# A two-layer hybrid decoder on one core: the first MLP's up half as seven block products, and its modulation vectors summed beside the first stages

## The chip, the cores and the metric

The kernel runs on one core of one Trainium2 chip. The metric is the device time of one execution in microseconds (us), the median of several. TensorE (PE in the profile) does the matrix products; VectorE (DVE), ScalarE (ACT) and GpSimd (POOL) work on its results; SyncE (SP) issues most of the DMAs. Each engine works through its own list of instructions in order and waits on semaphores for the others.

## The reference

One sequence of 1024 tokens of width 1024 goes through two layers. Cut to what matters here (`modulate` is x * (1 + scale) + shift):

```python
cs = silu(c)
sh_m, sc_m, g_m, sh_f, sc_f, g_f = split(cs @ ada_w[layer] + ada_b[layer], 6)
kv_shift, kv_scale = split(cs @ kv_ada_w + kv_ada_b, 2)          # once, for the shared K and V
# layer 0: y = mlstm_mixer(modulate(h, sh_m, sc_m)); layer 1: y = sliding-window attention over shared K and V
h = layer_norm(ALPHA * h + (1 + g_m) * y, ln_g[2 * layer], ln_b[2 * layer])
u = modulate(h, sh_f, sc_f)
y = square(relu(u @ mlp_w_up[layer])) @ mlp_w_down[layer]        # 1024 -> 4096 -> 1024
h = layer_norm(ALPHA * h + (1 + g_f) * y, ln_g[2 * layer + 1], ln_b[2 * layer + 1])
```

Fourteen vectors of 1024 entries come out of the `cs @ ada_w` products: six for each layer (named SH_M0 ... G_F0 and SH_M1 ... G_F1) and SH_KV and SC_KV for the shared K and V.

## The kernel before

**Products.** Every fp32 product is done as three products of rounded parts: high by high, high by low, low by high (`product`, L2670 to L2672). So each operand is split into a high part (ACT, L964 for weights) and a low part (DVE, L1609 for weights: the whole less the high part).

**Stages, in order.** A start; the q and k projection; the projection to v (16 tiles of 24 products, "V tiles", evacuated by DVE in `evac_v`, L1761, from a ring of three PSUM banks); the o projection with the mLSTM chunks between, whose first state product is L2914; the mixer's output (out0, out1); the first MLP (MLP0); K and V (KV); q and attention; the attention's output (op0, op1); the second MLP (MLP1).

**The two MLPs.** Each goes through the 4096 inner columns in 8 chunks of 512. Chunk 0 is done plainly: 8 up groups of 24 products and 16 down groups of 12. For the other chunks the matrices are cut into 2 by 2 blocks and multiplied with seven block products in place of eight (P1 to P7; their operands are sums and differences of blocks). MLP1 does so in the up half and in the down half (`both_chunk`, 168 + 168 products; its last chunk has plain downs), with the low parts of the summed u operands stored in DRAM and fetched back through a ring (`ulo_dram`). MLP0 does so in the down half alone (`seven_chunk`, 192 + 168 products in chunks 1 to 6), and its chunk 7 is plain.

**Vectors.** A vector needs eight row blocks of `ada_w` (512 KB each), which SP fetches into one of two slots of `stage`; DVE adds each, times its entry of cs, to `acc` (`ada`, L1567 and L1571: one of them is called an ada here), and PE then sums over the partitions (`sum_vector`, or `sum_quarters`, L2695, and `turn_quarters` in MLP0); `take_mod` (L1591) reads the sum. Weights pass through the same two slots of `stage`, in one order (`load_order`). Three vectors are summed beside the q, k and v projections (SH_F0, SC_F0, SH_KV), two in the mixer's later stages (G_M0, G_F0), and the seven others beside MLP0's chunks 0 to 6. A slot comes free when the piece in it has been used on DVE, and only then does SP issue its next load.

**Attention.** It goes through 16 pairs p. For each, DVE reads the sums of the exponentials (`totals`, L2308 and L2309, twice for each pair), POOL scales the probabilities (L890), and PE transposes them (L3149). For p of 8 and more DVE also does `affine_kv` (L2323, L2324: the norm's row times and plus a tile of the residual).

**Last chunk of MLP1.** The row `ln_b` is added to the tiles of the residual: to four by POOL (L923) during the ups, to four by DVE (L2650) during the downs. In MLP0 the row is added in chunk 0 by DVE (`affine`, L1981 and L1982).

## Time and profile before

| | before |
|---|---|
| median of 3 runs | 2147.69 us (2147.02 to 2148.5) |
| the profiled execution | 2148.5 us, its span 2146.8 us |
| PE busy | 2100.7 us, 98% of the span |
| DVE busy | 1502.8 us, 70% |
| ACT busy | 882.8 us, 41% |
| POOL busy | 270.6 us, 13% |
| mean granted clock of TensorE | 0.997 |

The span is the profiled stretch from the first to the last instruction; every start time below is counted from its beginning. A row of the timeline gives the start, the duration, engine, line, operation, result and operands, the number of instructions, and in brackets the idle time of the engine before it with what ended it. A result in PSUM is written by PE, and the engine that reads it frees the bank.

### The profile page before, as it was taken

What the parts mean: (1) busy time and instruction counts of PE and PEld (TensorE: products, weight loads), DVE (VectorE), ACT (ScalarE), POOL (GpSimd) and SP (SyncE); (2) the same over time, 40 slices, a digit from 0 to 9 for tenths busy, and PEclk for the clock granted to TensorE, in tenths of its full rate; (3) what the DMA queues carried; (4) which work ended last, traced back from release to release, by engine and by line L of the source; (5) the groups of instructions that cost most, each with busy time, mean ns of one, the idle gap of its engine ahead of it and who ended that gap; (6) DMA issues with size and microseconds to landing.
All of it is one profiled execution on the core that took longest, in us unless ns stands there. A gap on an engine that the chain in (4) does not pass through costs nothing.

```text
span 2146.8 us, 28666 instructions
## 1 busy us (share of the span) xinstructions
PE 2100.7 (98%) x9816; PEld 1702.2 (79%) x9816; DVE 1502.8 (70%) x2343; ACT 882.8 (41%) x1529; POOL 270.6 (13%) x248
## 2 busy tenths in 40 slices
PE   6999999999999999999999999999999999999998
PEld 5888888878888888888888777678787888888886
DVE  7423666678676676776768665767788788778878
ACT  4201454162234233342337455655434434534552
POOL 0000220010010110110100023232000011011034
PEclk9999999999999999999999999999999999999999
DMA  7434643303424224224121210211345433533531
GB/s 298 137 102 126 124 94 139 126 20 120 126 69 137 97 79 137 78 83 147 34 98 72 79 30 11 79 58 42 124 182 185 162 131 137 205 114 121 195 137 79
DMA packets 77315, 242.16 MB, mean 113 GB/s; under 512 B 8417, under 2 KB 8593, under 8 KB 73649
## 3 DMA queue, kind: packets, MB, share of 16 engines
q1 hardware_dynamic: 69376, 219.18, 30.1%
q0 software_dynamic: 5088, 17.48, 3.7%
q10 hardware_dynamic: 2768, 4.41, 0.5%
q8 instruction: 50, 0.82, 0.2%
q14 instruction: 33, 0.26, 0.0%
HBM read 225.29 MB, written 15.76 MB: 112 GB/s over the span
## 4 chain that ended last, share of the span: by engine, by line
PE 84%; DVE 7%; DMA 4%; ACT 3%; issue 2%; POOL 1%; SPq 0%; DVEq 0%; ACTq 0%; POOLq 0%
PE ps L2670 25%; PE ps L2672 25%; PE ps L2671 25%; DMA stage<-in_stream 3%; PE ps L3135 1%; PE ps L3165 1%; PE ps L3149 1%; DVE wlo L1609 1%; ACT whi L964 1%; PE ps L2914 1%; PE ps L2773 1%; PE ps L2899 1%; DMA early_place<-in_early 1%; PE ps L2903 1%; DVE stats L1918 1%
## 5 line engine op out<-in xcount | busy, mean ns | idle before, releaser
L2672 PE MATMUL ps<-uhi,wlo 128*128 128x512 f32 x760 | 296.4, 390 | 0.0
L2670 PE MATMUL ps<-whi,uhi 128*128 128x512 f32 x704 | 287.6, 408 | 0.2 <-ACT resid L1309 0.2
L2670 PE MATMUL ps<-uhi,whi 128*128 128x512 f32 x704 | 276.3, 392 | 5.9 <-DVE wlo L1609 3.2
L2672 PE MATMUL ps<-whi,ulo 128*128 128x512 f32 x704 | 275.4, 391 | 0.0
L2671 PE MATMUL ps<-wlo,uhi 128*128 128x512 f32 x704 | 274.8, 390 | 0.0
L2671 PE MATMUL ps<-ulo,whi 128*128 128x512 f32 x704 | 274.8, 390 | 0.0
L2672 PEld LDWEIGHTS ps<-uhi,wlo 128*128 128x128 f32 x760 | 143.1, 188 | 29.8
L2670 PEld LDWEIGHTS ps<-uhi,whi 128*128 128x128 f32 x704 | 132.6, 188 | 37.0 <-DVE wlo L1609 4.6
L2670 PEld LDWEIGHTS ps<-whi,uhi 128*128 128x128 f32 x704 | 132.5, 188 | 36.6 <-issue 10.0
L2672 PEld LDWEIGHTS ps<-whi,ulo 128*128 128x128 f32 x704 | 132.2, 188 | 28.9
L2671 PEld LDWEIGHTS ps<-ulo,whi 128*128 128x128 f32 x704 | 132.5, 188 | 27.2
L2671 PEld LDWEIGHTS ps<-wlo,uhi 128*128 128x128 f32 x704 | 132.6, 188 | 24.9
L2107 DVE TENSOR_TENSOR resid<-ps,resid 128x512 f32<-128x512 f32 x168 | 112.4, 687 | 50.9 <-PE ps L2672 50.9
L964 ACT ACTIVATE whi<-stage 128x1024 fp32r<-128x1024 f32 x76 | 79.3, 1053 | 148.5 <-DMA stage<-in_stream 54.2
L1609 DVE TENSOR_TENSOR wlo<-stage,whi 128x1024 fp32r<-128x1024 f32 x76 | 92.8, 1230 | 65.7 <-ACT whi L964 65.3
L1571 DVE SCALAR_TENSOR_TENSOR acc<-stage,cs,acc 128x1024 f32<-128x1024 f32 x84 | 107.6, 1281 | 43.5 <-DMA stage<-in_stream 42.3
L2471 DVE TENSOR_TENSOR resid<-ps,resid 128x512 f32<-128x512 f32 x168 | 109.2, 681 | 11.3 <-PE ps L2672 10.7
L1219 ACT ACTIVATE h_blocks<-ps 128x512 f32<-128x512 f32 x48 | 28.6, 595 | 211.6 <-PE ps L2672 211.6
L2670 PE MATMUL ps<-whi,hhi 128*128 128x512 f32 x288 | 113.1, 393 | 0.2
L2671 PE MATMUL ps<-wlo,hhi 128*128 128x512 f32 x288 | 112.1, 389 | 0.0
L2672 PE MATMUL ps<-whi,hlo 128*128 128x512 f32 x240 | 93.5, 389 | 0.0
L866 POOL TENSOR_TENSOR whi<-w_whole,wlo 128x1024 fp32r<-128x1024 f32 x12 | 28.9, 2407 | 496.2 <-DVE hhi L2071 486.1
(437 smaller groups left out, 4614.6 us busy)
## 6 DMA issues: line engine op xcount, KB each, us to landing
stage<-in_stream SPq DMA_DIRECT2D x248, 512.0 KB, 3.6
hlo<-ulo_dram SPq DMA_DIRECT2D x28, 1024.0 KB, 4.8
ulo<-ulo_dram SPq DMA_DIRECT2D x20, 1024.0 KB, 5.3
w_whole<-in_stream SPq DMA_DIRECT2D x14, 512.0 KB, 5.2
aux<-in_early SPq DMA_DIRECT2D x8, 512.0 KB, 7.5
...
```

The costliest lines, as they stand in the source:

```text
L866: pool.tensor_tensor(w_part(lo), w_block(lo), fr(w_part(hi)), ALU.subtract).then_inc(w_low_by_pool, 1)
L964: act.activation(whi[:, slot_of(w), :], stage[:, n % 2, :], ACT.Copy).then_inc(hi_ready, 1)
L1219: act.activation(block, ps[:, g % RING, :], ACT.Relu).then_inc(act_evac, 1)
L1571: ins = v.scalar_tensor_tensor(acc[:], stage[:, n % 2, :], cs[:, 0, k:k + 1], acc[:], ALU.mult, ALU.add)
L1609: v.tensor_tensor(wlo[:, slot_of(w), :], stage[:, n % 2, :], fr(whi[:, slot_of(w), :]), ALU.subtract).then_inc(loads_used, 1)
L1918: return v.bn_stats(stats[:, t % 2, 6 * half:6 * half + 6], resid[:, t, half * HALF:(half + 1) * HALF])
L2107: v.tensor_tensor(dst, ps[:, bank, :], dst, ALU.add).then_inc(dve_evac, 1)
L2471: v.tensor_tensor(dst, ps[:, down_bank(first, product, t), :], dst, ALU.add).then_inc(dve_evac, 1)
L2670: pe.matmul(dst, left_hi, right_hi, start=start, stop=False, skip_group_check=more)
L2671: pe.matmul(dst, left_hi, right_lo, start=False, stop=False, skip_group_check=more)
L2672: return pe.matmul(dst, left_lo, right_hi, start=False, stop=stop, skip_group_check=more)
L2773: last = pe.transpose(ps[:, X + n % 4, k * P:(k + 1) * P], src[:, at:at + P], ident[:])
```

## The change

1. **MLP0 by seven products in both halves.** MLP0's chunks 1 to 6 are done by the code of MLP1 (`both_chunk`, now with the MLP's number m as an argument), and chunk 7 has seven-product ups and plain downs as in MLP1. The stores and ring loads of `ulo_dram` and the four-part loads of blocks are issued by SP in MLP0 too. `seven_chunk`, `sum_quarters` and `turn_quarters` are gone.
2. **Vectors.** SH_F0, SC_F0 and SH_KV are summed beside the blocks 7 to 13 of the weights (during the q and k projection); SC_KV, SH_M1, SC_M1 and G_M1 beside the V tiles 1 to 15, two adas in a tile (three, three and two in the last tiles); SH_F1 and SC_F1 one ada in every V tile, whose pieces are fetched to a buffer of their own (`scratch`, one slot, with its own semaphores `side_in` and `side_used`), called side loads here; G_F1 beside the second half of the o projection. Every vector is summed with `sum_vector`.
3. **First chunks of the MLPs.** The weights come in the order 2, 3, 4, 5, 6, 7 (before: 4, 5, 2, 3, 6, 7), the first of them right behind the square of the third up group.
4. **Modulations.** `angles` and the modulations 2 to 4 move from MLP0's end to the first tiles of out1.
5. **Attention.** The first `totals` of each pair stands ahead of `affine_kv`.
6. **P2's weight.** In every `both_chunk` the low part of P2's weight (`both_up_low`) stands ahead of the gates 0 and 1 (a gate multiplies a block of the down weight by the gate row).
7. **The row ln_b.** POOL adds it to all eight tiles in the last chunk of both MLPs.

The core of the diff:

```diff
+SIDE = (SH_F1, SC_F1)
+BESIDE_QK = {7: [(SH_F0, 0, 3)], 8: [(SH_F0, 3, 6)], 9: [(SH_F0, 6, 8)], 10: [(SC_F0, 0, 4)], 11: [(SC_F0, 4, 8)],
+             12: [(SH_KV, 0, 4)], 13: [(SH_KV, 4, 8)]}
+BESIDE_V = {t: (v, 2 * n, 2 * n + 2) for first, v in ((1, SC_KV), (5, SH_M1), (9, SC_M1)) for n, t in
+            enumerate(range(first, first + 4))}
+BESIDE_V.update({13: (G_M1, 0, 3), 14: (G_M1, 3, 6), 15: (G_M1, 6, 8)})
-CHUNK_LOADS = [4, 5, 2, 3, 6, 7, 8, 9]
+CHUNK_LOADS = [2, 3, 4, 5, 6, 7]
+LOADS_AT = {2: (2,), 3: (3, 4), 4: (5,), 5: (6,), 6: (7,)}
...
+            def load_one(n):
+
+                sp.wait_ge(loads_used, n - 1)
+                sp.dma_start(stage[:, n % 2, :], stream[n]).then_inc(stage_loaded[n % 2], 16)
+
+            def load_side(n):
+
+                if n:
+                    sp.wait_ge(side_used, n)
+                else:
+                    sp.wait_ge(gate_m, 6)
+                sp.dma_start(scratch[:].rearrange("p a n -> p (a n)"), stream[SIDE_BASE + n]).then_inc(side_in, 16)
+
+            load_pairs(2, IN_V, 0)
+            load_side(0)
+            tile = 1
+            for n in range(IN_V, AFTER_V):
+                load_one(n)
+                while tile < 2 * T and n + 1 >= LOADED_THROUGH[tile - 1]:
+                    load_side(tile)
+                    tile += 1
+            load_pairs(AFTER_V, N_EARLY, 0)
...
-            for t in range(T):
-                adas(SC_F0, range(t, t + 1))
-                if t == T - 1:
+            for tile in range(2 * T):
+                nh, t = divmod(tile, T)
+                if tile == T - 1:
                     preps(14, 15)
-                evac_v(0, t)
-            for t in range(T):
-                evac_v(1, t)
-                adas(SH_KV, range(t, t + 1))
...
+                evac_v(nh, t)
...
+                ada(SIDE[nh], t)
+                if tile in BESIDE_V:
+                    adas(*BESIDE_V[tile])
...
-                if p >= T:
-                    affine_kv(p - T)
                 if more:
                     totals(2 * p + 2)
+                if p >= T:
+                    affine_kv(p - T)
+                if more:
                     totals(2 * p + 3)
...
-            mlp_chunk(FIRST["mlp0"], W_MLP0, 0, with_ada=True, head=lambda t: normed(TR_LN0, 0, t))
-            with pe.Fori(0, len(SEVEN)) as i:
-                seven_chunk(chunk_start(FIRST["mlp0"], 1), W_MLP0 + 8, 0, i, 16, True)
+            def mlp_through(m, tail=None):
+
+                mlp_chunk(m)
+                with pe.Fori(0, len(SEVEN)) as i:
+                    both_chunk(m, both_start(FIRST[MLP[m]], 1), 0, i)
+                first = both_start(FIRST[MLP[m]], CHUNKS - 1)
+                both_chunk(m, first, len(SEVEN), 0, last=True)
```

How the instructions stand now. The first place is DVE in the V tiles of before: between two evacuations (L1761) stands one ada (L1571), which reads a slot of `stage`.

```order
L1761 COPY resid<-ps 128x2x256
L1571 SCALAR_TENSOR_TENSOR acc<-stage,cs,acc 128x1024
L1761 COPY resid<-ps 128x2x256
L1571 SCALAR_TENSOR_TENSOR acc<-stage,cs,acc 128x1024
L1761 COPY resid<-ps 128x2x256
```

The same place of the changed kernel, where the evacuation is L1743, an ada L1556 or L1560, and the second vector's total lies in `gate_row`:

```order
L1743 COPY resid<-ps 128x2x256
L1570 TENSOR_TENSOR mods<-ps,mods 128x8
L1560 SCALAR_TENSOR_TENSOR acc<-scratch,cs,acc 128x1024
L1560 SCALAR_TENSOR_TENSOR gate_row<-stage,cs,gate_row 128x1024 x2
L1743 COPY resid<-ps 128x2x256
L1560 SCALAR_TENSOR_TENSOR acc<-scratch,cs,acc 128x1024
L1560 SCALAR_TENSOR_TENSOR gate_row<-stage,cs,gate_row 128x1024 x2
```

Between two evacuations there now stand three adas: one that reads the side load (`scratch`) and two that read the slots of `stage`.

On SP the loads of this stretch were one loop over pairs of `stage` loads. In the changed kernel they are written out behind that loop, from V tile 1 on:

```order
L708 DMA scratch<-in_stream 128x1024
L700 DMA stage<-in_stream 128x1024 x2
L708 DMA scratch<-in_stream 128x1024
L700 DMA stage<-in_stream 128x1024 x2
L708 DMA scratch<-in_stream 128x1024
```

So one side load follows each two `stage` loads, in one queue; a side load waits until the side piece before it is used, and a `stage` load until its slot is free.

The second place is DVE in the pair p = 8 of attention, before: the low parts of two weights, `affine_kv` (L2323, L2324), then `totals` twice (L2308, L2309) and the low part of the output (L2316).

```order
L1609 TENSOR_TENSOR wlo<-stage,whi 128x1024 x2
L2323 TENSOR_TENSOR resid<-resid,lnrows 128x1024
L2324 TENSOR_TENSOR resid<-resid,acc 128x1024
L2308 TENSOR_TENSOR att<-att 128x4
L2309 RECIPROCAL att<-att 128x4
L2308 TENSOR_TENSOR att<-att 128x4
L2309 RECIPROCAL att<-att 128x4
L2316 TENSOR_TENSOR ulo<-ps,uhi 128x4x128
```

The same pair of the changed kernel:

```order
L1588 TENSOR_TENSOR wlo<-stage,whi 128x1024 x2
L2399 TENSOR_TENSOR att<-att 128x4
L2400 RECIPROCAL att<-att 128x4
L2414 TENSOR_TENSOR resid<-resid,lnrows 128x1024
L2415 TENSOR_TENSOR resid<-resid,acc 128x1024
L2399 TENSOR_TENSOR att<-att 128x4
L2400 RECIPROCAL att<-att 128x4
L2407 TENSOR_TENSOR ulo<-ps,uhi 128x4x128
```

The first of the two `totals` has moved ahead of `affine_kv`, the second has stayed behind it.

The third place is DVE in MLP1's chunk 0, before: behind each square (L1997) the weight's scaling (L1604), the low part of the up group (L2001), the low part of a weight (L1609) and a row of the residual (L2611). The weights are 4 and 5; weight 2, which the fifth up group needs, comes right behind these rows.

```order
L1997 TENSOR_TENSOR h_whole<-h_whole 128x512
L1604 TENSOR_TENSOR stage<-stage,gate_row 128x1024
L2001 TENSOR_TENSOR hlo<-h_whole,hhi 128x512
L1609 TENSOR_TENSOR wlo<-stage,whi 128x1024
L2611 TENSOR_TENSOR resid<-resid,lnrows 128x1024
L1997 TENSOR_TENSOR h_whole<-h_whole 128x512
L1604 TENSOR_TENSOR stage<-stage,gate_row 128x1024
L2001 TENSOR_TENSOR hlo<-h_whole,hhi 128x512
L1609 TENSOR_TENSOR wlo<-stage,whi 128x1024
L2611 TENSOR_TENSOR resid<-resid,lnrows 128x1024
L1997 TENSOR_TENSOR h_whole<-h_whole 128x512
L2001 TENSOR_TENSOR hlo<-h_whole,hhi 128x512
```

The same place of the changed kernel, where the square is L1985 and the low part of a weight L1588:

```order
L1985 TENSOR_TENSOR h_whole<-h_whole 128x512
L1992 TENSOR_TENSOR hlo<-h_whole,hhi 128x512
L2235 TENSOR_TENSOR resid<-resid,lnrows 128x1024
L1985 TENSOR_TENSOR h_whole<-h_whole 128x512
L1992 TENSOR_TENSOR hlo<-h_whole,hhi 128x512
L2235 TENSOR_TENSOR resid<-resid,lnrows 128x1024
L1985 TENSOR_TENSOR h_whole<-h_whole 128x512
L1588 TENSOR_TENSOR wlo<-stage,whi 128x1024
L1992 TENSOR_TENSOR hlo<-h_whole,hhi 128x512
```

Weight 2 is now the first of the chunk, behind the third square, and the two scaled weights have moved behind it.

## Rows read from the trace of the kernel before

**Rows 1.** The page, busy time of the engines, share of the span
```profile
PE 2100.7 (98%) x9816; PEld 1702.2 (79%) x9816; DVE 1502.8 (70%) x2343; ACT 882.8 (41%) x1529; POOL 270.6 (13%) x248
```

**Rows 2.** Windows: PE, PEld, DVE, ACT, POOL busy (instructions), granted clock, DMA share, GB/s
```profile
129.88:221.24 91.36, 90.58 (x415) 75.10 (x414) 35.32 (x41) 8.39 (x18) 2.80 (x4) 1.00 0.41 121
466.00:1117.91 651.91, 649.56 (x2909) 531.94 (x2909) 461.49 (x559) 220.62 (x296) 62.09 (x33) 1.00 0.31 98
1498.51:2110.22 611.71, 604.86 (x2656) 497.34 (x2657) 492.28 (x541) 277.61 (x358) 64.90 (x35) 1.00 0.42 149
```

**Rows 3.** Timeline of PE: chunk starts in MLP1 and MLP0
```profile
1749.88 0.39 PE L2670 MATMUL ps<-uhi,ninth 128*128 128x512 f32 x1
1826.14 0.39 PE L2670 MATMUL ps<-uhi,ninth 128*128 128x512 f32 x1
...
714.11 0.64 PE L2695 MATMUL ps<-acc,ones 128*32 128x256 f32 x8
797.01 0.64 PE L2695 MATMUL ps<-acc,ones 128*32 128x256 f32 x8
```

**Rows 4.** Timeline and window of MLP1's chunk 0
```profile
1525.88 1.23 DVE L1609 TENSOR_TENSOR wlo<-stage,whi 128x1024 fp32r<-128x1024 f32 x1 [0.25 <-ACT whi L964]
...
1527.16 0.50 PE L2670 MATMUL ps<-uhi,whi 128*128 128x512 f32 x1 [2.75 <-DVE wlo L1609]
...
1527.16:1531.60 4.44, 4.44 (x12) 3.53 (x13) 3.49 (x4) 1.58 (x2) 0.00 (x0) 0.62 0.40 122
```

**Rows 5.** Timeline and window of attention's pair 8
```profile
1358.43 1.22 DVE L2323 TENSOR_TENSOR resid<-resid,lnrows 128x1024 f32<-128x1024 f32 x1
1359.68 1.23 DVE L2324 TENSOR_TENSOR resid<-resid,acc 128x1024 f32<-128x1024 f32 x1
...
1363.22 1.09 PE L3149 MATMUL ps<-ident,probs 128*128 128x128 f32 x8 [3.13 <-POOL probs L890]
...
1363.22:1368.60 5.38, 5.38 (x24) 3.67 (x26) 2.58 (x15) 1.17 (x3) 2.40 (x2) 0.68 0.13 25
```

**Rows 6.** Timeline of DVE: four adas in a row, then a V tile
```profile
97.43 1.28 DVE L1571 SCALAR_TENSOR_TENSOR acc<-stage,cs,acc 128x1024 f32<-128x1024 f32 x1
100.99 1.28 DVE L1571 SCALAR_TENSOR_TENSOR acc<-stage,cs,acc 128x1024 f32<-128x1024 f32 x1 [2.28 <-DMA stage<-in_stream]
103.19 1.28 DVE L1571 SCALAR_TENSOR_TENSOR acc<-stage,cs,acc 128x1024 f32<-128x1024 f32 x1 [0.91 <-DMA stage<-in_stream]
105.83 1.28 DVE L1571 SCALAR_TENSOR_TENSOR acc<-stage,cs,acc 128x1024 f32<-128x1024 f32 x1 [1.36 <-DMA stage<-in_stream]
...
141.11 0.70 DVE L1761 COPY resid<-ps 128x512 f32<-128x512 f32 x1 [3.56 <-PE ps L2672]
```

**Rows 7.** The tile stage, 90 to 130 us: its loads, issue to landing
```profile
DMA to landing us min/median/max: 3.4/3.5/4.3
```

**Rows 8.** Timeline of PE: a vector's sum, and the first state product
```profile
128.18 1.84 PE L2687 MATMUL ps<-ones,acc 128*128 128x1 f32 x16
129.88 0.49 PE L2670 MATMUL ps<-whi,uhi 128*128 128x512 f32 x1
...
228.41 0.70 PE L2914 MATMUL ps<-resid,ktok 128*128 128x257 f32 x2 [0.26 <-DVE mods L1591]
```

**Rows 9.** Waits of PE: result, line, what ended them, total, times, longest
```profile
PE ps L2670 <- DVE h_blocks L2441: 1.3, 2, 0.8
...
PE ps L2670 <- DVE spare_r L2411: 0.7, 1, 0.7
...
PE ps L2670 <- DMA ulo<-ulo_dram: 0.5, 1, 0.5
```

**Rows 10.** Timeline of POOL and DVE in MLP1's last chunk
```profile
2068.52 12.55 POOL L923 TENSOR_TENSOR resid<-resid,lnrows 128x1024 f32<-128x1024 f32 x4 [7.11 <-ACT lnrows L1453]
...
2079.33 2.83 DVE L2411 TENSOR_TENSOR whi<-w_whole,hhi 128x1024 fp32r<-128x1024 f32 x1
...
2090.08 1.22 DVE L2452 TENSOR_TENSOR hhi<-h_blocks,wlo 128x1024 fp32r<-128x1024 f32 x1
```

1642 lines of the change are left out of this document (707 added, 935 removed).

## The prediction

> **What bounds the kernel now.** The first view was the page: PE is busy for 98% of the span, no other engine for more than 70% [rows 1]. So the time is PE's instructions plus its few waits, and a change pays by products removed or waits removed. Next came the windows of the stages: in MLP0, in MLP1 and in the V tiles PE is busy all the time but for a few us [rows 2]. Then the waits of PE one by one: most are under 1 us [rows 9], two are near 3 us [rows 4, 5]. Last I read DVE and the loads where the change adds work [rows 6, 7], since there PE's cover decides.
>
> **MLP0.** A product starts each 76.26 / 336 = 0.227 us: in MLP1 a chunk of 336 products lasts from 1749.88 to 1826.14. In MLP0 a chunk of 360 lasts 82.90 us (714.11 to 797.01) [rows 3]; 24 products are 5.45 us of the 6.64 between, the vector's quarter sums the rest, 1.2 us. Chunks 1 to 7 lose 24 products each: 168 × 0.227 = 38.1 us, and chunks 0 to 6 their sums, 7 × 1.2 = 8.4 us: 46.5. A direct comparison says the same with MLP1's stalls in it: from the first product to the end of the third tile of the last downs MLP0 takes 651.91 us, MLP1, which is what MLP0 becomes, 611.71 [rows 2]. MLP1's number holds 4.6 us that the change removes (next part): 607.1. Term: **−44.8 us**. The change to P2's order concerns the entry from chunk 0 to chunk 1: there PE waits 0.7 us for a weight's low part, then 0.5 for a ring load, then up to 0.8 for an addition of DVE [rows 9]. The first goes away; but the ring load is issued by PE's progress and lands no earlier, so the next wait takes it over. I count 0 in either MLP, bounds −1.5 and +1.5.
>
> **MLP1's chunk 0.** PE waits 2.75 us for weight 2's low part, and its next 12 products take 4.44 us at a granted clock of 0.62 where 12 × 0.227 = 2.7 would do [rows 4]. In the new order DVE has four instructions of 1.22 us less ahead of that low part, and needs only about 3.4 us to be in time. Term: −2.9 − 1.7 = **−4.6 us**; the bound above is 0.
>
> **Attention, pair 8.** DVE does `affine_kv` (1.22 + 1.23 us) ahead of `totals`; PE waits 3.13 us for the probabilities, and the next 5.38 us run at 0.68, which costs 5.38 × 0.32 = 1.7 us [rows 5]. With `totals` ahead, 2.4 us of the wait go and, the wait being short then, I take it that the clock stays up. Term: **−4.1 us**; bounds −4.8 and −2.4.
>
> **The vectors beside q, k and V.** This is where time is given back. *PE's part:* a vector's sum takes 129.88 − 128.18 = 1.70 us [rows 8]; eleven are made where there were four, six of the seven new ones ahead of the first state product (L2914 at 228.41 [rows 8]), which gives +10.2, and one in out0, +1.7. *The loads' part:* before, each V tile has one ada, and DVE waits 3.56 us for PE in a tile [rows 6]. After, a tile has two adas from `stage`, one from the side buffer. Where before four adas follow each other, DVE waits for the loads: two adas start each 105.83 − 100.99 = 4.84 us [rows 6], because a slot must be used, then filled (3.5 us from issue to landing [rows 7]). So two loads need 4.84 us of the 5.45 of a tile, and everything else that passes through `stage` comes on top. I count the chain from 97.43, behind the low part of weight 10: 19 `stage` loads up to weight 13 and the last of SH_KV, 37 from there to weight 18, 56 × 2.42 = 135.5 us; eight of them are weights, whose slot is held until ACT's high part (1.05 us) and DVE's low part are made, about +1.16 each, 9.3; and about 4.6 us from the last weight's landing to the state product, for DVE's and ACT's other work. That gives 97.4 + 149.4 = 246.8. The side load stands in the same queue and shares the DMA engines; where loads follow each other closely their landing rises from 3.5 to 4.3 us [rows 7], so each of 15 side loads may delay the others by 0 to 0.8 us: 246.8 to 258.8. I take the middle, 252.5: **+24 us** against 228.41. The bounds: +10.2 (PE alone binds), and +36 (landing at 4.3 for each pair, and a little of DVE's order lost). The Trainium skill ("DMA: Bandwidth & Descriptors", Anatomy of one DMA — SWDGE (gpsimd) path) has 2.0 us + bytes / 436e3 for one DMA, an estimate of 3.2 us for 512 KB. By that rule only 1.2 us of a load is transfer and a third load in flight costs next to nothing, so the stretch would end at 246.8, 6 us sooner. The trace's 3.5 us is near the rule, its 4.3 speaks against the second half of it.
>
> **The clock in that stretch.** A PE that waits for loads may wait 3 us or more at a time; after the two waits of that size the clock fell for 4.4 and 5.4 us at a cost of 1.7 each [rows 4, 5]. I count two such: **+3.5 us**, bounds 0 and +10.
>
> **The adds on POOL.** While POOL does its four adds (12.55 us), DVE's additions of two SBUF operands take 2.83 us where they take 1.22 soon after [rows 10]. Now eight adds stand in the last ups of both MLPs. Each further add costs DVE about 1.6 us, 4 × 1.6 = 6.4 us in MLP1, and in MLP0 as much beyond what the 611.71 holds, and DVE's idle time beside the ups and the four adds that it loses hide most. I take 1.5 us for each: **+3 us**, bounds 0 and +10. The Trainium skill ("SBUF — State Buffer", Terms) calls the port pair of DVE and GpSimd exclusive, held for the full instruction; the trace agrees, 2.83 against 1.22 us. By it all of the 6.4 us is lost where DVE has no idle time, +12.8 for both, which would make the sum 10 us longer.
>
> **At no cost:** the modulations in out1 and the first chunk's other moves, behind which DVE waits for PE in each tile; if that cover were gone, a modulation would be worth 1 to 2 us once. The copy in place of a zeroed state is as long.
>
> **Sum,** against the profiled execution's own 2148.5 us: −44.8 −4.6 −4.1 +24 +1.7 +3.5 +3 = −21.3, so 2127.2. The median of the runs shown is 0.8 lower than that execution: **2126.4 us**, 1.0% faster.
>
> **The rivals.** *(a) The loads fit under PE.* If a side load hides wholly and the weights' stage time overlaps, the stretch costs PE's sums alone, +10.2 and no clock loss: 2126.4 − 13.8 − 3.5 = 2109. For it: 4.84 us for two loads is under 5.45. Against it: the weights and the long runs of four adas in the q and k projection, where before already DVE waits for loads. Chance 0.13. *(b) The stretch is much slower.* Landing at 4.3 or more with three loads in flight, DVE's order holding up PE, more clock loss: +36 and +7, 2142. Chance 0.12. *(c) POOL's lock.* By the rule above all of DVE's lost time shows: 2136. Chance 0.08. *(d) The other side: the side loads run in series with the stage loads.* SP issues in order; a side load waits until DVE has used the one before, and DVE uses it only behind an evacuation that waits for PE. If so each stage load behind it starts only then, and a tile needs three loads in turn, 3 × 2.42 = 7.3 us or more: 71 loads × 2.42 = 172 + 13.9, the state product at 283, +55, 2157. Against it: when a side load is issued, its slot was freed a tile before, at the head of DVE's adas. It decides from about 6.7 us per V tile (16 tiles × 1.3 = 21 us, which eats the gain). Chance 0.04. *(e) The change of P2's order and POOL's eight adds do nothing at all:* 2123, inside my own range. Chance of my case (2119 to 2134): 0.63.
>
> **How the numbers follow.** The forecast is the likeliest, 2126. Leaving out the ends of (a) and (b), the range 2110 to 2140 holds 8 in 10: its low end is (a), its high end takes in (c) and most of (b); my own case has 2119 to 2134. A measurement of this kernel can tell about 0.2%, 4.3 us. Faster (under 2143.4): cases (a), (c), mine and most of (b), 0.93; within 0.2%: 0.03, from the end of (b); slower: 0.04, case (d).
>
> **What would show each step.** MLP0 from first product to the third tile's end near 607 us, chunks at 76.3; no wait for weight 2 in MLP1's chunk 0; at pair 8 a wait under 1 us and a clock of 1.0; the first state product between 245 and 259, with PE waits in the V tiles that end in DVE's copy or adas, and DVE waits that end in `stage` or `scratch` DMA; V tiles of 6 us rather than 5.45; DVE's additions at 2.8 us for some 25 us in both last ups. The prediction is wrong above all if the V tiles take 5.5 us or over 6.7.

## The result and the profile after

The changed kernel takes 2197.18 us (median of 4 runs, 2193.72 to 2201.87), the kernel before 2148.1 us beside it (4 runs): a ratio of 1.0229, interval 1.0209 to 1.0249. It is 2.3% slower; forecast was 2126, 1.0% faster. Two executions with a lower granted clock and a much longer time, one of e2's (3923.67 us) and one of the kernel before (3542.37 us), are left out of every number.

The page of the changed kernel, its first part, to be set beside [rows 1]:

```profile
span 2195.5 us, 28565 instructions
PE 2092.7 (95%) x9676; PEld 1691.5 (77%) x9676; DVE 1617.8 (74%) x2406; ACT 942.2 (43%) x1594; POOL 302.1 (14%) x255
```

PE is busy for 8 us less in a span 48.7 us longer: PE stands idle longer, and behind its waits products run at a lower granted clock. The waits of PE (total us, how often, the longest one) name where; [rows 9] has those of before:

```profile
PE ps L2509 <- DVE h_blocks L2065: 18.7, 24, 1.7
PE ps L2529 <- DVE gate_row L1560: 15.9, 3, 10.8
PE ps L2697 <- DVE resid L1743: 5.9, 1, 5.9
PE ps L2966 <- DVE att L2383: 5.3, 6, 2.6
PE ps L2509 <- DVE wlo L1588: 5.0, 3, 2.1
PE ps L2599 <- DVE qk L1783: 3.1, 2, 2.4
PE ps L2529 <- DVE acc L1560: 2.9, 1, 2.9
```

`L2509` with `h_blocks` is mostly the group of products P6 (one of the seven of an up half), `L2529` a vector's sum, `L2697` a group of transposes whose bank a V tile's evacuation has yet to free. All the releasers are DVE instructions, none is a load; what DVE itself waited for has to be read from its own timeline.

To divide the 48.7 us, I took the start of one instruction at the edge of each stage in both traces (us from the start of the span):

| stage, up to | before | after | the stage is longer by | forecast |
|---|---|---|---|---|
| q/k projection: first product of V tile 0 | 129.88 | 132.91 | +3.0 | 0 |
| V tiles: first state product | 228.41 | 277.74 | +46.3 | +24 with the clock's +3.5 apart |
| mLSTM chunks: first transpose for the o projection | 330.09 | 380.03 | +0.6 | 0 |
| o projection: MLP0's first product | 466.00 | 531.52 | +15.6 | +1.7 |
| MLP0: first transpose of the KV stage | 1168.88 | 1203.83 | −30.6 | −44.8, adds +1.5 |
| KV stage: first score | 1230.43 | 1265.40 | 0.0 | 0 |
| attention: MLP1's first product | 1498.51 | 1537.63 | +4.2 | −4.1 |
| MLP1: last matmul | 2137.20 | 2185.93 | +9.6 | −4.6, adds +1.5 |

Every stage that holds a part of the change comes out worse than its term.

**The V tiles.** PE's timeline: the first product of V tile 0, the three longest waits (in brackets), and the first state product:

```profile
132.91 0.49 PE L2509 MATMUL ps<-whi,uhi 128*128 128x512 f32 x1
154.93 3.57 PE L2529 MATMUL ps<-ones,gate_row 128*128 128x1 f32 x16 [10.84 <-DVE gate_row L1560]
241.94 3.57 PE L2529 MATMUL ps<-ones,gate_row 128*128 128x1 f32 x16 [4.44 <-DVE gate_row L1560]
265.04 2.07 PE L2697 MATMUL ps<-qk 128*128 128x128 f32 x8 [5.85 <-DVE resid L1743]
277.74 0.70 PE L2742 MATMUL ps<-resid,ktok 128*128 128x257 f32 x2 [0.26 <-DVE mods L1570]
```

DVE's timeline in and around it (the number before `DMA` is DVE's idle time):

```profile
126.11 1.28 DVE L1560 SCALAR_TENSOR_TENSOR acc<-stage,cs,acc 128x1024 f32<-128x1024 f32 x1 [6.66 <-DMA stage<-in_stream]
153.59 1.28 DVE L1560 SCALAR_TENSOR_TENSOR gate_row<-stage,cs,gate_row 128x1024 f32<-128x1024 f32 x1 [1.48 <-DMA stage<-in_stream]
154.79 0.68 DVE L1743 COPY resid<-ps 128x512 f32<-128x512 f32 x1
198.49 1.23 DVE L1588 TENSOR_TENSOR wlo<-stage,whi 128x1024 fp32r<-128x1024 f32 x1 [3.98 <-ACT whi L1000]
254.98 1.28 DVE L1560 SCALAR_TENSOR_TENSOR gate_row<-stage,cs,gate_row 128x1024 f32<-128x1024 f32 x1 [6.86 <-DMA stage<-in_stream]
```

The ada of 153.59 is the last piece of SH_KV, and V tile 0's evacuation (`L1743`) stands directly behind it. PE stood for 10.84 us ahead of SH_KV's sum; that the sum itself then lasts 3.57 us where it takes 1.70 [rows 8] is the clock's price. The waits of 6.66 and 6.86 us have a neighbour: POOL fetches `decay_rows` and `dmat` just ahead of both (the first pair, POOL's timeline) in pieces of 512 bytes. The 6.86 us lie ahead of PE's wait of 5.85.

```profile
114.06 0.80 POOL L847 DMA_DIRECT2D decay_rows<-rows_dram  x1 [2.48 <-DMA rows_dram<-winter]
114.85 0.76 POOL L847 DMA_DIRECT2D dmat<-rows_dram  x1
```

The windows of the V stretch and of the o projection (length, busy time of PE, PEld, DVE, ACT, POOL, granted clock, DMA share, GB/s):

```profile
132.91:277.74 144.83, 118.57 (x539) 98.98 (x538) 86.74 (x91) 12.93 (x27) 5.34 (x6) 0.88 0.73 230
380.03:531.52 151.49, 142.09 (x661) 116.88 (x660) 100.73 (x190) 53.83 (x100) 10.28 (x23) 0.97 0.34 107
```

PE is idle for 26.3 us in the first, where the 98.53 us of before held 1.1 us of waits in all. Its mean clock is 0.88, and a part of the waits is paid again in slower products: PE's busy time grew by 21.1 us (97.49 before), five more sums at 1.70 us [rows 8] are 8.5 of it, and the other 12.6 us are an estimate of what the lower clock cost. In the second stretch PE is idle for 9.4 us; the longest waits are these (and two for `wlo`, 1.02 us at 480.61 and 1.83 us at 484.10):

```profile
421.50 1.85 PE L2599 MATMUL ps<-ident,qk 128*128 128x128 f32 x8 [2.40 <-DVE qk L1783]
444.40 2.54 PE L2529 MATMUL ps<-ones,acc 128*128 128x1 f32 x16 [2.93 <-DVE acc L1560]
```

**Attention, pair 8.** The wait of [rows 5], 3.13 us, is down to 1.66, and others stand beside it. POOL, DVE and PE:

```profile
1393.85 2.79 POOL L938 TENSOR_TENSOR probs<-probs,att 128x1024 f32<-128x1024 f32 x1 [5.54 <-DVE att L2400]
1393.67 1.21 DVE L2414 TENSOR_TENSOR resid<-resid,lnrows 128x1024 f32<-128x1024 f32 x1
1394.92 2.80 DVE L2415 TENSOR_TENSOR resid<-resid,acc 128x1024 f32<-128x1024 f32 x1
1396.69 1.09 PE L2980 MATMUL ps<-ident,probs 128*128 128x128 f32 x8 [1.66 <-POOL probs L938]
1400.34 2.08 PE L2966 MATMUL ps<-kt,resid 64*128 64x256 f32 x8 [2.56 <-DVE att L2383]
1400.00:1406.00 6.00, 5.67 (x22) 3.57 (x22) 3.37 (x13) 1.40 (x5) 0.59 (x1) 0.61 0.25 87
```

With `totals` first, POOL's product of the probabilities starts earlier and so falls on `affine_kv`: the product takes 2.79 us and DVE's second step 2.80, where [rows 5] has 1.23 for the latter. PE still waits 1.66 us for the product. DVE comes 1.6 us later to the next maxima, and PE waits 2.56 us there, with a clock of 0.61 around it (last line, a window). In the whole of attention the waits for maxima are 5.3 us in six places, where they were 0.4 in two.

**The MLPs.** The same product of two chunks in a row in MLP1, and P6's wait between them; then what DVE does ahead of the addition that P6 waits for:

```profile
1786.85 0.39 PE L2509 MATMUL ps<-uhi,ninth 128*128 128x512 f32 x1
1809.72 0.50 PE L2509 MATMUL ps<-ulo,wlo 128*128 128x512 f32 x1 [0.79 <-DVE h_blocks L2065]
1864.33 0.39 PE L2509 MATMUL ps<-uhi,ninth 128*128 128x512 f32 x1
1800.23 1.22 DVE L2048 TENSOR_TENSOR w_whole<-stage,gate_row 128x1024 f32<-128x1024 f32 x1 [2.67 <-DMA stage<-in_stream]
1808.98 0.68 DVE L2065 TENSOR_TENSOR h_blocks<-ps,h_blocks 128x512 f32<-128x512 f32 x1
```

A chunk takes 77.48 us where [rows 3] has 76.26, and so it is in every steady chunk of both MLPs (77.3 to 77.8, from eleven). Ahead of the addition at 1808.98 DVE waits 2.67 us and 0.70 us for two gates' loads, and six sums, low parts and gates of 1.22 us lie between. In the last chunks, with POOL's eight adds, the products wait six times for such additions and not once; MLP1's and MLP0's:

```profile
PE ps L2509 <- DVE h_blocks L2065: 4.4, 6, 1.6
PE ps L2509 <- DVE h_blocks L2065: 4.4, 6, 1.7
```

### The profile page after: what moved, and what is told of

Same layout as the page of the kernel before. It is cut to its first block, busy times and chain, and to the rows that moved or that the text cites. A ratio compares the mean times of both kernels' runs of the same rounds, so it can differ in the third digit from the quotient of the medians.

```text
span 2195.5 us, 28565 instructions
## 1 busy us (share of the span) xinstructions
PE 2092.7 (95%) x9676; PEld 1691.5 (77%) x9676; DVE 1617.8 (74%) x2406; ACT 942.2 (43%) x1594; POOL 302.1 (14%) x255
## 4 chain that ended last, share of the span: by engine, by line
PE 69%; DVE 13%; DMA 10%; issue 3%; ACT 3%; SPq 1%; POOL 1%; DVEq 0%; ACTq 0%; POOLq 0%
PE ps L2509 21%; PE ps L2511 20%; PE ps L2510 20%; DMA stage<-in_stream 9%; PE ps L2966 1%; PE ps L2996 1%; DVE wlo L1588 1%; DVE w_whole L2058 1%; DVE whi L2035 1%; DVE gate_row L1560 1%; DVE acc L1560 1%; DVE w_whole L2048 1%; PE ps L2980 1%; ACT whi L1000 1%; DVE ulo L1879 1%
## 5 line engine op out<-in xcount | busy, mean ns | idle before, releaser
L2509 PE MATMUL ps<-whi,uhi 128*128 128x512 f32 x704 | 293.3, 417 | 5.2 <-DVE wlo L1588 5.0
L2509 PEld LDWEIGHTS ps<-whi,uhi 128*128 128x128 f32 x704 | 135.3, 192 | 42.9 <-issue 10.0
L2510 PEld LDWEIGHTS ps<-wlo,uhi 128*128 128x128 f32 x704 | 135.5, 192 | 25.6
L2511 PE MATMUL ps<-uhi,wlo 128*128 128x512 f32 x368 | 143.5, 390 | 0.0
L1588 DVE TENSOR_TENSOR wlo<-stage,whi 128x1024 fp32r<-128x1024 f32 x68 | 83.0, 1232 | 58.4 <-ACT whi L1000 57.9
L2509 PE MATMUL ps<-whi,ninth 128*128 128x512 f32 x288 | 112.0, 389 | 0.0
L2048 DVE TENSOR_TENSOR w_whole<-stage,gate_row 128x1024 f32<-128x1024 f32 x56 | 71.7, 1300 | 48.7 <-DMA stage<-in_stream 48.7
L2509 PE MATMUL ps<-uhi,whi 128*128 128x512 f32 x256 | 101.4, 396 | 2.6 <-DVE ulo L1879 1.4
L2510 PE MATMUL ps<-ulo,whi 128*128 128x512 f32 x256 | 100.1, 391 | 0.0
L1258 ACT ACTIVATE h_blocks<-h_blocks 128x512 f32<-128x512 f32 x84 | 52.4, 624 | 95.9 <-DVE h_blocks L2065 95.9
L2509 PE MATMUL ps<-uhi,wlo 128*128 128x512 f32 x224 | 87.7, 392 | 4.2 <-DVE h_blocks L2065 3.6
L2065 DVE TENSOR_TENSOR h_blocks<-ps,h_blocks 128x512 f32<-128x512 f32 x84 | 57.4, 684 | 45.8 <-PE ps L2511 45.8
L2509 PE MATMUL ps<-ulo,hhi 128*128 128x512 f32 x224 | 87.5, 391 | 1.4 <-DVE h_blocks L2065 1.4
L2510 PE MATMUL ps<-hlo,wlo 128*128 128x512 f32 x224 | 87.3, 390 | 0.0
L2511 PE MATMUL ps<-uhi,spare_r 128*128 128x512 f32 x224 | 87.3, 390 | 0.0
```

Source lines behind the costliest of these rows:

```text
L1258: act.activation(part, part, ACT.Relu).then_inc(inner_relu, 1)
L1588: v.tensor_tensor(wlo[:, slot_of(w), :], stage[:, n % 2, :], fr(whi[:, slot_of(w), :]), ALU.subtract).then_inc(loads_used, 1)
L2048: v.tensor_tensor(place((B12, B22, B11, B21)[j]), src, row, ALU.mult).then_inc(loads_used, 1)
L2065: v.tensor_tensor(part, ps[:, up_bank(first, UPS[slot], f), :], part, ALU.add).then_inc(dve_evac, 1)
L2509: pe.matmul(dst, left_hi, right_hi, start=start, stop=False, skip_group_check=more)
L2510: pe.matmul(dst, left_hi, right_lo, start=False, stop=False, skip_group_check=more)
```

## The experiments

Each ratio is against the kernel before, run beside it; a time without a ratio is a single run. Lengths of stages are between the instructions of the table above; "V stretch" is the second row. A stage whose code is unchanged differs from run to run: the V stretch took 143.8 to 147.1 us in the changed kernel and in e1 to e4 and e7, the o projection 148.7 to 153.8 in those that keep G_F1 there. My first account of the loss was: three loads in a V tile are too many; P2's order delays P6 in every chunk; the adds on POOL cost more than 3 us; `totals` ahead moves the wait; G_F1's loads push the o projection back. Each has the rival that the part costs nothing and the time is lost elsewhere.

**e1, P2's low part back behind the gates 0 and 1**

```diff
                 both_up_low(m, "P4", q, i)
-                both_up_low(m, "P2", q, i)
                 gate(0)
                 gate(1)
+                both_up_low(m, "P2", q, i)
                 gate(2)
```

> The changed kernel with one thing undone: P2's weight's low part stands behind the gates 0 and 1 again. Theory A (the order on DVE is the cost): the low part ahead of the gates pushes the gates and sums of the down weights back, and with them DVE's addition on which P6 waits; the chunks of both MLPs, 77.6 us in the changed kernel, go back to 76.3, so 12 steady chunks and the two last ones give 14 to 19 us: 2197 becomes 2178 to 2183. Rival B (the longer chunk comes from the DMA traffic or from POOL, in MLP0 and MLP1 alike, and not from this order): the chunks stay at 77.6 and the time within 3 us of 2197.

2183.25 us, ratio 1.017 (1.0153 to 1.0187): −14 against the changed kernel. Steady chunks start 76.2 us apart again, and between 1525 and 1850 us, where MLP1's first chunks are, no wait for `h_blocks` is left. MLP0 is 5.1 us shorter, MLP1 9.1. The order costs 14.2 us beside the other edits; I had counted 0.

**e2, `totals` back behind `affine_kv`**

```diff
-                if more:
-                    totals(2 * p + 2)
                 if p >= T:
                     affine_kv(p - T)
                 if more:
+                    totals(2 * p + 2)
                     totals(2 * p + 3)
```

> The changed kernel with one thing undone: both totals stand behind affine_kv again. Theory A (the wait only moved: POOL's product now runs beside DVE's affine_kv, both are stretched, and DVE comes late to the next maxima): attention goes back to what it took before, the 4.2 us that it now takes longer come back: 2197 becomes 2193, with one wait for the probabilities of 3.1 us and none of 2.6 us for the maxima. Rival B (attention is longer for another reason, such as the loads): it stays at 2197 or gets slower by the 2.4 us that the order should have saved.

2192.54 us (3 runs), ratio 1.0208 (1.0188 to 1.0229): −4.6, near what runs differ by. The stage itself says it better: attention takes 268.0 us, as before the change (268.1), against 272.2, with the waits of before: one of 3.1 us for the probabilities and 0.4 in all for maxima. The reorder costs 4.2 us.

**e3, POOL adds ln_b to four tiles and DVE to four, in both MLPs**

```diff
-                for t in range(T):
+                for t in range(T // 2):
                     pool.tensor_tensor(resid[:, t, 0:D], resid[:, t, 0:D], lnrows[:, 1, :],
...
+                    if nh == 0 and t < T // 2:
+                        whole = resid[:, T // 2 + t, 0:D]
+                        v.wait_ge(rows_ready, (2, 5)[m])
+                        v.tensor_tensor(whole, whole, lnrows[:, 1, :], ALU.add).then_inc(h_by_dve, 1)
```

> The changed kernel with POOL adding the row ln_b to four tiles in the last chunk of each MLP and DVE to four, during the downs, as MLP1 had it before. Theory A (POOL's eight adds stretch DVE's additions of two SBUF operands all through the last ups, and PE waits six or seven times there): the waits of PE in the last ups, together 6.8 us in MLP1 and 7.3 in MLP0 beyond the pitch, shrink to about 2 each: 2197 becomes 2186 to 2190. Rival B (the waits there come from P2's order alone and from the low parts' order): under 2 us of change.

2193.33 us, ratio 1.0221 (1.0204 to 1.0238), 3.9 less than the changed kernel, where 7 to 11 was expected; the intervals of the two overlap. MLP0 is 3.4 us shorter, MLP1 3.5.

**e4, all three of these at once** (the edits of e1, e2 and e3)

> The changed kernel with all three of the edits before: P2 behind the gates, both totals behind affine_kv, four adds on POOL and four on DVE. If the three costs are separate the savings add up: 16 + 4 + 9 = 29 us, 2168, still 20 us over the kernel before, all of it ahead of MLP0 (the first state product 49 us later, out0 and out1 16 us longer, MLP0 shorter by 45). If the adds' waits and P2's order are one cost seen twice, the sum is smaller, about 2173.

2165.5 us, ratio 1.0087 (1.007 to 1.0103): −31.7. That is more than −14, −4.6 and −3.9 together. The stages say where: the MLPs are 13.7 and 15.5 us shorter, 29.2 in all, where e1 gave 14.2 and e3 6.8. The other 8 us go only when both are undone, and they lie in the last chunks: from its first product `uhi,ninth` to the last matmul MLP1's last chunk takes 82.3 us before, 89.0 in the changed kernel, 89.0 in e1, 85.8 in e3 and 82.3 in e4. So the two costs overlap there: as long as one edit is in place DVE stays late, and undoing the other gives little. In e1, where only the adds are left, DVE goes from step to step without a pause from 2099.9 to 2125 us while POOL adds, and PE waits at the end of it (POOL, DVE, PE):

```profile
2095.49 25.85 POOL L918 TENSOR_TENSOR resid<-resid,lnrows 128x1024 f32<-128x1024 f32 x8 [7.12 <-ACT lnrows L1307]
2116.31 2.82 DVE L2076 TENSOR_TENSOR whi<-w_whole,wlo 128x1024 fp32r<-128x1024 f32 x1
2123.08 0.56 PE L2509 MATMUL ps<-uhi,wlo 128*128 128x512 f32 x1 [3.57 <-DVE h_blocks L2065]
```

With both gone MLP0 takes 658.6 us and MLP1 632.8, that is −44.3 and −5.9 against before; the terms −44.8 and −4.6 stand, and what was wrong in the MLPs is the price of the order and of the adds.

**e5, the 16 side loads and their adas left out**

```diff
             def load_side(n):

+                return
                 if n:
...
                 if vec in SIDE:
+                    if k == 0:
+                        v.memset(total, 0.0).then_inc(side_used, K)
+                    return
```

> The changed kernel without the 16 side loads and their adas (the vectors SH_F1 and SC_F1 are left at their bias, the rest is unchanged). Theory A (three loads for a V tile are too many; two fit under a tile's 5.45 us): the first state product, at 277.7 us in the changed kernel and 228.4 in the one before, comes at 252 to 260; what remains is the wait of 11 us for SH_KV's sum at 155 and the collisions with other loads. Rival B (the side loads run beside the others and cost next to nothing; the q and k projection's chain and the collisions are all): 273 or later.

2197.76 us, and the V stretch is 141.6 us long against 144.8. The long wait is nearly as long as in the changed kernel:

```profile
154.64 3.57 PE L2533 MATMUL ps<-ones,gate_row 128*128 128x1 f32 x16 [10.34 <-DVE gate_row L1564]
```

The theory that a third load in a tile is what is too much falls, and with it any price for the loads of SH_F1 and SC_F1 much beyond 3 us.

**e6, the side loads of 64 KB instead of 512 from the second on**

```diff
-                sp.dma_start(scratch[:].rearrange("p a n -> p (a n)"), stream[SIDE_BASE + n]).then_inc(side_in, 16)
+                size = D if n == 0 else P
+                sp.dma_start(scratch[:].rearrange("p a n -> p (a n)")[:, 0:size],
+                             stream[SIDE_BASE + n][:, 0:size]).then_inc(side_in, 16)
```

> The changed kernel with side loads of an eighth of the bytes from the second on (64 KB in place of 512; the adas as they were, so the values of SH_F1 and SC_F1 are others). If the side loads cost by their transfer, the first state product comes within 4 us of where the kernel without side loads has it; if they cost by DVE's time and by the order on SP's queue, it stays within 4 us of 277.7. Theory A takes the first for two thirds of the difference.

2200.15 us, V stretch 143.8 us, 1.0 less, no more than runs differ by. The bytes of the side loads aren't it either.

**e7, G_F1's eight loads and adas left out**

```diff
-        ada(*BESIDE_O1[t])
+        pass
     w(28, 29)
-    for t in range(T - 1):
+    for t in range(2, T - 1):
         ada(*BESIDE_OUT0[t])
...
```

> The changed kernel without G_F1's eight loads and adas beside the second half of the o projection and out0 (the vector is left at its bias, its sum on PE stays). From the first transpose of hs to MLP0's first product the changed kernel takes 151.5 us, the one before 135.9. Theory A (G_F1 shifts the o projection's weights and G_F0's adas back, and with them out0 and out1): 139 to 142. Rival B (the modulations and angles in out1, and G_F1's sum on PE, are the cost): 148 or more.

2192.5 us. The o projection takes 141.0 us against 151.5: some 10.5 of the 15.6 us lost there are those of G_F1's loads and adas. Of the total only 4.7 us show, since in this run the V stretch was 147.1 us long and the MLPs 3 us longer. Two waits of the changed kernel for low parts (`wlo`) are left, 1.04 and 1.82 us.

**e8, the rows that POOL fetches laid out by chunk, so that they come in pieces of 2 KB**

```diff
-                pool.dma_start(rows_dram[w], src[:]).then_inc(rows_out, 16)
-            pool.wait_ge(rows_out, 32)
+                for h in range(H):
+                    pool.dma_start(rows_dram[w].rearrange("(t h) n -> h t n", h=H)[h],
+                                   src[h * T:(h + 1) * T, :]).then_inc(rows_out, 16)
+            pool.wait_ge(rows_out, 32 * H)
...
-                src = rows_dram[w].rearrange("(h t) n -> t h n", t=T)[c]
+                src = rows_dram[w].rearrange("(t h) n -> t (h n)", h=H)[c]
...
```

> The changed kernel with the decay rows laid out in DRAM by chunk, so that a chunk's four heads lie side by side and POOL's two fetches for a chunk read pieces of 2 KB in place of 512 bytes, the same 512 KB in all. Theory A (the waits of 6.7 us at 119 and 6.9 us at 248 for a stage load come from these fetches, which fill the DMA engines with small pieces): both waits shrink to under 4 us and the first state product comes 5 to 9 us earlier, 2197 becomes 2188 to 2192. Rival B (the load is late because of the bytes in flight, whatever their pieces, or for another reason): under 2 us of change.

2192.13 us, ratio 1.0212 (1.0189 to 1.0235), which overlaps the changed kernel's interval; the waits are clearer. DVE's two waits of 6.66 and 6.86 us for a `stage` load are gone, the longest from 95 us to the state product is 3.06. PE's waits in the V stretch:

```profile
PE ps L2531 <- DVE gate_row L1562: 11.4, 3, 6.9
PE ps L2699 <- DVE resid L1745: 3.3, 1, 3.3
```

The longest wait fell from 10.8 to 6.9 us, the one for an evacuation from 5.9 to 3.3. The first state product starts 6.2 us sooner (271.53). Same bytes, larger pieces: the form of another queue's fetches was worth some 5 to 6 us of the stage loads.

**e9, the vectors placed by room.** On e4 and e8: SH_F1, SC_F1 and G_F1 are summed beside the q turns and the first pairs of attention, SH_M1 and SC_M1 take the side buffer, block 13 has no piece and V tiles have at most two `stage` pieces.

```diff
-SIDE = (SH_F1, SC_F1)
+SIDE = (SH_M1, SC_M1)
...
-             12: [(SH_KV, 0, 4)], 13: [(SH_KV, 4, 8)]}
-BESIDE_V = {t: (v, 2 * n, 2 * n + 2) for first, v in ((1, SC_KV), (5, SH_M1), (9, SC_M1)) for n, t in
-            enumerate(range(first, first + 4))}
-BESIDE_V.update({13: (G_M1, 0, 3), 14: (G_M1, 3, 6), 15: (G_M1, 6, 8)})
-BESIDE_O1 = {t: (G_F1, t - 2, t - 1) for t in range(2, 8)}
+             12: [(SH_KV, 0, 2)], 13: []}
+BESIDE_V = {0: (SH_KV, 2, 4), 1: (SH_KV, 4, 6), 2: (SH_KV, 6, 8), 3: (SC_KV, 0, 1), 4: (SC_KV, 1, 3),
+            5: (SC_KV, 3, 5), 6: (SC_KV, 5, 6), 7: (SC_KV, 6, 7), 8: (SC_KV, 7, 8), 9: (G_M1, 0, 1), 10: (G_M1, 1, 2),
+            11: (G_M1, 2, 4), 12: (G_M1, 4, 5), 13: (G_M1, 5, 7), 14: (G_M1, 7, 8)}
...
+BESIDE_TURNS = {0: (SH_F1, 0, 2), 1: (SH_F1, 2, 4), 2: (SH_F1, 4, 6), 3: (SH_F1, 6, 8), 6: (SC_F1, 0, 2),
+                7: (SC_F1, 2, 4)}
+BESIDE_PAIRS = {0: (SC_F1, 4, 6), 1: (SC_F1, 6, 8), 3: (G_F1, 0, 2), 4: (G_F1, 2, 4), 5: (G_F1, 4, 6), 6: (G_F1, 6, 8)}
...
```

> A version on the fourth experiment (three edits undone) with the wide rows of the eighth, and with the vectors placed otherwise: SH_F1, SC_F1 and G_F1 are summed beside the turns of q and the first seven pairs of attention, where `stage` is idle; SH_M1 and SC_M1 take the side loads, one piece in each V tile; `stage` carries 2 pieces at most in a V tile (22 in place of 32 and the weights), and two less beside blocks 12 and 13. Theory C (the two slots of `stage` are the limit: about 2.8 us for a piece in the V tiles, and the side slot beside them is nearly free): the first state product comes at 236 to 248 us (278.5 in the fourth experiment), from there to MLP0's first product about 238 us as before the change, and the whole is 2118 to 2135, faster than the kernel before. Rival D (the V tiles are slow because a third stream of adas and loads, whoever issues them, crowds DVE and the DMA engines, so that moving pieces within the stretch does not help): the state product stays beyond 262. Rival E (the adas in attention delay the probabilities as affine_kv did): attention grows by 5 us or more beyond its three sums, 5.1 us.

2139.75 us (8 runs), ratio 0.9963 (0.9951 to 0.9976): faster than the kernel before, by 0.4%, and above the expected 2118 to 2135. The first state product comes at 238.7 us, inside its range. The V stretch takes 106.1 us (before 98.5, changed 144.8), the o projection 139.5 (135.9, 151.5), MLP0 657.8, MLP1 633.1. But attention takes 292.5 where it took 268.1: rival E was right. Its waits:

```profile
PE ps L3002 <- DVE att L2413: 9.5, 2, 9.2
PE ps L3016 <- POOL probs L958: 6.3, 3, 3.1
```

The 9.2 us end at 1232.98, and just ahead, from 1222, DVE has a run of four adas that wait 1.8, 1.9 and 0.8 us for their loads, with an evacuation among them and the next pair's maxima behind them: the same fault in a new place.

**e10, the kernel before with the new order of loads in MLP1's chunk 0 alone**

```diff
+NEW_LOADS = [2, 3, 4, 5, 6, 7]
+LOADS_AT = {2: (2,), 3: (3, 4), 4: (5,), 5: (6,), 6: (7,)}
...
-    w(*[W_MLP1 + j for j in CHUNK_LOADS[:6]])
+    w(*[W_MLP1 + j for j in NEW_LOADS])
```

> The kernel before with one part of the change alone: in MLP1's chunk 0 the weights come in the order 2, 3, 4, 5, 6, 7, the first behind the third square. By the trace the wait of 2.75 us for weight 2 and the slow products behind it go: 4.6 us, 2147.9 becomes 2143.3, ratio 0.998. Rival: the scaled weights 4 to 7, now later, are waited for in their turn (PE waits for DVE's low part of weight 7 ahead of the first down group), and the time stays within 1.5 us.

2144.38 us (10 runs), ratio 0.9979 (0.997 to 0.9988): −3.7. MLP1 takes 633.95 us where it took 638.69, so 4.7 in the stage; the term was −4.6.

**e11, e9 with SC_F1 and G_F1 spread otherwise over attention** (the diff is against e9; the sums move too, SH_F1's ahead of attention's first score, and the scaling of weights 108 and 109 goes behind the `totals`)

```diff
-                7: (SC_F1, 2, 4)}
-BESIDE_PAIRS = {0: (SC_F1, 4, 6), 1: (SC_F1, 6, 8), 3: (G_F1, 0, 2), 4: (G_F1, 2, 4), 5: (G_F1, 4, 6), 6: (G_F1, 6, 8)}
+BESIDE_TURNS = {0: (SH_F1, 0, 2), 1: (SH_F1, 2, 4), 2: (SH_F1, 4, 6), 3: (SH_F1, 6, 8), 5: (SC_F1, 0, 2)}
+BESIDE_PAIRS = {0: (SC_F1, 2, 4), 1: (SC_F1, 4, 6), 2: (SC_F1, 6, 8), 4: (G_F1, 0, 3), 5: (G_F1, 3, 6), 6: (G_F1, 6, 8)}
```

> The ninth experiment's version with the adas in attention moved away from its start: SC_F1's pieces two beside the turn 5 and two beside each of the pairs 0 to 2, G_F1's beside the pairs 4 to 6, the sums one pair later, and the scaling of weights 108 and 109 behind the totals. In the ninth experiment attention took 24 us longer than before the change, 5.1 of it for three sums, 9.2 in one wait for the maxima at the pair 0, where DVE waited for loads, and about 2 at each of two waits for the probabilities. Theory (those waits are DVE's waits for loads ahead of maxima and totals): 10 to 16 us come back, 2139.8 becomes 2124 to 2130. Rival (any ada beside attention delays it, wherever it stands): less than 5 us come back, waits of the same size at other pairs.

2137.97 us (5 runs), ratio 0.9953 (0.9939 to 0.9967), a miss: 10 to 16 us were expected. By the marks attention is 6.6 us shorter (285.9), but the stage ahead of it, K and V, is 3.9 us longer (65.4 against 61.5), since SH_F1's sum, with a wait of 1.85 us ahead of it, now stands in front of the first score. Both stages together are 2.8 us shorter, and the one wait of 9.2 us has turned into several small ones:

```profile
PE ps L3021 <- POOL probs L960: 7.5, 4, 3.1
PE ps L3007 <- DVE att L2415: 4.4, 5, 2.3
```

The median moved by 1.8 us only; the intervals of e9 and e11 overlap, so that e11 beats e9 isn't shown.

**e12, SC_M1's eight pieces left out of `stage`; e13, the last four of SH_KV; e14, both and e8's rows.** After e5 the cause of the V stretch was open: one chain of loads in which each costs the same (as forecast), or single places that are too full. All three are single runs.

```diff
-        if tile in BESIDE_V:
+        if tile in BESIDE_V and BESIDE_V[tile][0] != SC_M1:
             ada(*BESIDE_V[tile])
...
-        for part in BESIDE_QK[block]:
+        for part in BESIDE_QK[block] if block < 13 else ():
             ada(*part)
```

> The changed kernel without the eight `stage` loads and adas of SC_M1 beside the V tiles 9 to 12 (the vector is left at its bias, its sum on PE stays); the side loads stay. In the fifth experiment 16 side pieces were left out and the first state product came 3 us sooner. Theory C (the two slots of `stage` are what the V tiles wait for, 2.8 us for a piece): half as many pieces, from `stage`, bring it 14 to 22 us sooner, from 277.7 to 256 to 264. Rival D (DVE's time and the DMA traffic, to which a side piece adds as much as a stage piece): 2 us sooner.

> The changed kernel without the last four of SH_KV's loads and adas, those beside block 13 of the weights (the vector lacks half of its sum; everything else is as in the changed kernel). Theory F (the lost time comes from a few places where the pieces pinned to a block or a tile do not fit, and the first is the end of the q and k projection: SH_KV's last piece is used at 154.9 us, V tile 0's evacuation stands behind it on DVE, and PE waits 11 us for the sum): the wait at 155 goes, the V tiles start as before at 132 to 133, and the first state product comes 9 to 13 us sooner, at 265 to 269. Rival (the chain of stage loads is one queue, and what is gained at its head is given back at later tiles only in part or in full, since the later pieces wait as long as before): it comes 4 x 2.8 = 11 us sooner as well if nothing is given back, and less than 5 us if PE only waits later; so a gain of 9 or more with the later waits unchanged in size speaks for F.

> The changed kernel with three things together: without SH_KV's last four pieces, without SC_M1's eight stage pieces, and with the wide decay rows. Alone they brought the first state product 8.5 us sooner (SC_M1), 6.4 us (wide rows) and what the thirteenth run shows (some 11). Theory F (separate places, each with its own wait): they add up, about 26 us sooner, at 249 to 255; only the waits at the tile of weights 14 and 15 and at the last tiles are left, and the half-clock stretches behind the waits shrink too. Rival (one chain, so that the same wait is removed three times): 262 or later.

| | time | V stretch | per load left out |
|---|---|---|---|
| changed | 2197.18 | 144.8 | |
| e12, eight pieces fewer | 2191.06 | 137.5 | 0.9 |
| e13, four pieces fewer | 2187.74 | 134.7 | 2.5 |
| e8, none fewer | 2192.13 | 139.5 | |
| e14, all three | 2178.79 | 120.5 | |

With one chain each piece left out would give the same, 2.4 us. Eight pieces in the middle gave 7.3 us (the first state product 8.3 us sooner, where e12 expected 14 to 22 or 2: neither), four at the tile that V's first evacuation waits for gave 10.1 (12.3 sooner, as e13 expected), and none at all with other fetches 5.3. The three add up to 22.7 and together gave 24.3; by the state product they add up to 26.8 and gave 23.9. Within what runs differ by these are the same: three separate places. Waits of e13 (two rows), then of e14 (three), in the V stretch:

```profile
PE ps L2697 <- DVE resid L1743: 9.8, 1, 9.8
PE ps L2529 <- DVE gate_row L1560: 4.8, 3, 2.1
```

```profile
PE ps L2706 <- DVE resid L1750: 4.8, 1, 4.8
PE ps L2538 <- DVE mods L1577: 2.4, 1, 2.4
PE ps L2516 <- DVE wlo L1595: 2.0, 1, 2.0
```

In e13 the wait for SH_KV's sum is gone (no sum waits over 2.1 us), and 3.9 us come back at the transposes near the stretch's end (5.85 us before, 9.77 now), right where POOL's second pair of fetches is; in e14, where these come in large pieces, it is 4.8.

## Why the prediction was wrong

**The vectors beside q, k and V, +24: right in kind, wrong in size and in its model.** I named the stretch load-bound, and it is: of DVE's 58 us of idle time in the V stretch 34 end in a `stage` load and 13 in ACT's high part of a weight. The measured price is +49.3 up to the state product against +24 with +3.5 for the clock, beyond the upper bounds of rival (b), +36 and +7. The step that failed is the chain, "56 × 2.42 = 135.5 us". It spreads the loads evenly and lets PE's work go on beside them. But a piece is pinned to a block or a tile in DVE's order, and what stands behind it (an evacuation, a low part) waits with it; a fixed chain says what the loads need in all, not what a full place costs. At the head it was short too: by the chain SH_KV's last ada, the 19th load, ends at 146.9 us (97.4 + 19 × 2.42 + 3 × 1.16), and it ended at 154.9, since DVE waited 6.66 us for one load and the last three adas started 2.72 and 2.77 us apart, not 2.42. Shown: e13's four pieces cost 10.1 us, e12's eight 7.3, and the fetches of POOL, which I hadn't looked at, 5.3 (e8). The 0 to 0.8 us for each side load held (e5: 3.3 us for 16), but its upper end rests on a misreading: the 4.3 us of [rows 7] is the longest landing of its window, and nothing in that row ties it to how closely loads follow each other. The Trainium skill's rule that stands beside the sum ("DMA: Bandwidth & Descriptors", Anatomy of one DMA — SWDGE (gpsimd) path) is given there for DMAs that GpSimd issues, and these are SP's; what the prediction drew from it, that a third load in flight costs next to nothing, fits e5. Rival (d), the side loads in series, gave nearly the right time of the state product (283 against 277.7) by a mechanism that e5 excludes. The clock term was too low with the waits: +3.5 us for two waits, bounds 0 and +10, against a mean clock of 0.88 over 144.8 us, by the estimate above 12.6 us. No run measures the clock's part by itself.

**The o projection, "one in out0, +1.7".** Only PE's sum was costed. G_F1's eight loads and adas ahead of the projection's weights weren't; they cost some 10.5 us (e7). Of the other 5 us, 1.7 are PE's sum as forecast, which e7 keeps, and 2.8 are PE's two waits for low parts, at 480.6 and 484.1, which the kernel before doesn't have and e7 and e9 do. Why these are late was not tried. The modulations moved there, which I counted at 0, are not the reason: DVE reaches the first of them at 484.56, behind both waits, and PE waits no more than 0.6 us after it.

**P2's order, "I count 0 in either MLP, bounds −1.5 and +1.5".** I looked at the entry from chunk 0 to chunk 1, where a wait had been, and not at the loop's steady pass. There P2's low part now stands ahead of gates that release `stage` slots. Steady chunks take 77.5 us instead of 76.2; e1 gives 14.2 us back, and with the adds shared the order costs 22.4 (e3 less e4). MLP1's entry got no better: PE waits 1.4 us for `ulo` from the ring there, more than the 0.5 of before [rows 9].

**The adds on POOL, "+3 us".** That DVE's steps take 2.8 us beside POOL's adds was forecast rightly. The step that failed is that DVE's idle time and the four adds that it loses "hide most". With P2's order undone the adds cost 15.0 us (e1 less e4), beyond the bound of +10: 6.4 in MLP1, the whole of the 4 × 1.6 us, and 8.6 in MLP0. So hardly any of it was hidden, and not because P2's order had used up DVE's idle time, for in e1 that order is undone and DVE has none left beside the adds (2099.9 to 2125 us). That e3 alone gives only 6.8 is the overlap of the two costs. Rival (c), +12.8 in place of +3, was close for this term and far off for the total.

**Attention, −4.1.** The wait fell by 1.5 us, from 3.13 to 1.66, and not by the 2.4 forecast, since POOL's product itself took 2.79 us in place of 1.88. What is late next was asked of PE only. The product moved onto `affine_kv` and both got longer, DVE's step by 1.6 us, and PE waits at the next maxima, and the clock did not stay up (0.61): +4.2, and e2 gives it back. The step that failed is "With `totals` ahead, 2.4 us of the wait go".

**What was right.** MLP0 by seven products: −44.3 us with the order and the adds undone (e4), term −44.8. Weight 2's order: −4.7 in the stage (e10), term −4.6, and e4's MLP1 says −5.9 (the sum has 2.9 us for a wait that [rows 4] has at 2.75, which changes nothing).

The misses add up: 21.8 in the V stretch and its clock (49.3 − 27.5), 13.9 in the o projection, 25.4 in the MLPs (−21.0 measured, −46.4 forecast), 8.3 in attention, 69.4 of the 71 between 2126.4 and 2197.2.
